# A decoder layer's MLP in blocks of 336 tokens, with the inner layer of its last 736 tokens as seven block products for eight, and GpSimd making a third of the low parts

## The reference

```
x = layer_norm(x, ln_in)
proj = x @ w_in                        # 1024 -> 9 * 256
y = [rg-lru, gated conv, stick-breaking attention, pooling](proj)   # 4 x 256
x = layer_norm(ALPHA * x + y @ w_out, ln1)
h = square(relu(x @ w_ff1))            # 1024 -> 4096
x = layer_norm(ALPHA * x + h @ w_ff2, ln2)     # 4096 -> 1024
```

## Time and profile before

| | |
|---|---|
| time, 3 runs | 2442.67, 2443.44, 2443.89 us |
| profiled execution | span 2440.8 us, 36,724 instructions; the page gives no time of its own beside the span |
| TensorE matmul / weight load, busy | 99% / 96% of the span |
| Vector, ScalarE, GpSimd, busy | 65%, 53%, 10% |
| DMA | 351.64 MB, 144 GB/s on average |
| block 0 begins, block 3 begins, block 4 begins | 527, 1696, 2130 us |

### The profile page before, as it was taken

The page is one execution under the profiler, slowest core; times in us unless marked ns, Lnnn a source line. Parts: engine busy times, 40 slices in busy tenths (PEclk is TensorE's granted clock), DMA queues, the critical chain, the costliest instruction groups (busy, mean ns, idle before and its releaser), DMA issues.

```text
span 2440.8 us, 36724 instructions
## 1 busy us (share of the span) xinstructions
PE 2406.7 (99%) x13263; PEld 2331.5 (96%) x13263; DVE 1585.0 (65%) x2233; ACT 1286.6 (53%) x1982; POOL 243.0 (10%) x527
## 2 busy tenths in 40 slices
PE   7999999999999999999999999999999999999998
PEld 7999999999999999999999999999999999999998
DVE  7635662656777787777788777757655665764335
ACT  5466523555655745656555565554455555444432
POOL 0012320200001100011100111000122130000000
PEclk9999999999999999999999999999999999999999
DMA  8434554534444434444443443333566674343332
GB/s 257 153 108 143 159 174 138 184 111 130 162 134 139 142 110 144 150 129 144 128 124 117 137 141 124 125 122 114 182 187 187 209 234 134 120 136 117 112 118 83
DMA packets 141526, 351.64 MB, mean 144 GB/s; under 512 B 20625, under 2 KB 64146, under 8 KB 141218
## 3 DMA queue, kind: packets, MB, share of 16 engines
q1 hardware_dynamic: 128994, 312.88, 40.6%
q0 software_dynamic: 12352, 36.42, 4.7%
HBM read 300.11 MB, written 49.12 MB: 143 GB/s over the span
## 4 chain that ended last, share of the span: by engine, by line
PE 95%; DVE 2%; ACT 2%; DMA 1%; issue 1%; SPq 0%; DVEq 0%; ACTq 0%
PE PS L1136 22%; PE PS L1138 22%; PE PS L1137 22%; PE PS L874 5%; PE PS L872 5%; PE PS L873 5%; PE PS L942 2%; PE PS L964 1%; PE PS L932 1%; PE PS L963 1%; PE PS L1026 1%; PE PS L933 1%; PE PS L1056 1%; PE PS L1014 1%; PE PS L912 1%
## 5 line engine op out<-in xcount | busy, mean ns | idle before, releaser
L1440 ACT ACTIVATE w_hi_lo<-w_raw 128x1024 fp32r<-128x1024 f32 x240 | 252.7, 1053 | 283.5 <-PE PS L1138 277.3
L1136 PE MATMUL PS<-a_hi,w_hi_lo 128*128 128x416 f32 x1080 | 385.1, 357 | 1.3 <-DVE w_hi_lo L1995 1.3
L1138 PE MATMUL PS<-a_hi,w_hi_lo 128*128 128x416 f32 x1080 | 379.3, 351 | 0.0
L1137 PE MATMUL PS<-a_lo,w_hi_lo 128*128 128x416 f32 x1080 | 378.6, 351 | 0.0
L1995 DVE TENSOR_TENSOR w_hi_lo<-w_raw,w_hi_lo 128x1024 fp32r<-128x1024 f32 x240 | 292.6, 1219 | 58.1 <-ACT w_hi_lo L1440 55.9
L1136 PE MATMUL PS<-h_hi,w_hi_lo 128*128 128x416 f32 x824 | 294.6, 358 | 0.0
L1138 PE MATMUL PS<-h_hi,w_hi_lo 128*128 128x416 f32 x824 | 290.2, 352 | 0.0
L1137 PE MATMUL PS<-h_lo,w_hi_lo 128*128 128x416 f32 x824 | 289.4, 351 | 0.0
L2022 DVE TENSOR_TENSOR h_lo<-h_full,h_hi 128x416 fp32r<-128x416 f32 x160 | 94.6, 592 | 222.9 <-ACT h_hi L1455 222.8
L1136 PEld LDWEIGHTS PS<-a_hi,w_hi_lo 128*128 128x128 f32 x1080 | 203.0, 188 | 4.1 <-DVE w_hi_lo L1995 1.7
L1137 PEld LDWEIGHTS PS<-a_lo,w_hi_lo 128*128 128x128 f32 x1080 | 203.5, 188 | 2.1
(11 more groups left out here) (336 smaller groups left out, 5203.8 us busy)
## 6 DMA issues: line engine op xcount, KB each, us to landing
w_raw<-w_all SPq DMA_DIRECT2D x380, 512.0 KB, 3.5
proj_scratch<-stage SPq DMA_DIRECT2D x70, 208.0 KB, 1.9
k_rows<-kv_out SPq DMA_DIRECT2D x80, 128.0 KB, 4.0
v_hi_lo<-v_scratch SPq DMA_DIRECT2D x40, 256.0 KB, 4.1
x_scratch<-x_full SPq DMA_DIRECT2D x20, 416.0 KB, 2.9
x_residual<-x_scratch SPq DMA_DIRECT2D x5, 1664.0 KB, 7.6
pages<-ck SPq DMA_DIRECT2D x64, 128.0 KB, 2.2
pages<-ck POOLq DMA_DIRECT2D x64, 128.0 KB, 2.5
```

Of the source, the lines that this page charges most:

```text
L1136: pe.matmul(out, w_h, mh_[:, k, :], start=(g == 0), stop=False)
L1137: pe.matmul(out, w_h, ml_[:, k, :], start=False, stop=False)
L1138: ins = pe.matmul(out, w_l, mh_[:, k, :], start=False, stop=(g == KT - 1))
L1440: act.activation(halves(w_hi(n)), raw_halves(n), ACT.Copy).then_inc(s_wh, 1)
```

## The change

**Blocks.** The MLP now has `NA` = 4 blocks of `MB` = 336 tokens, and a last part of 736 tokens that is two blocks (4 and 5) of `HB` = 368. Steps of blocks 0 to 3 are as before, but for their width. In block 3 the out steps of block 4 (r = 56 to 63) are followed by those of block 5 (r = 64 to 71), and the last eight down steps by nothing. So both normalisations run beside block 3's end. `N_STEPS` is 306. Rows of the second normalisation are 112 tokens, three tiles a block, at r = 1, 3 and 5.

**GpSimd.** `BY_POOL` lists every third step from 12 to 225. The low parts of those 72 weights are made by GpSimd, at the place of its list where the attention slot of that step is; its semaphore is its own (`s_wlp`), and TensorE and SP (`load_weights`) wait for it there.

**The last part.** For the up layer the weights of two output tiles and two halves of the contracted dimension form a 2 x 2 matrix of blocks, and so do the two halves of x with the two token blocks. Seven products of such blocks, with sums and differences of weights and of x as operands, and sums of products give what eight products gave. There are 8 chunks (`N_CH`), each with two units of seven up products (`b_up`), then eight weight tiles of the down layer, plain, with two groups each (`b_down`, `b_down_last`). A product or a group is 12 matmuls of 368 columns (`b_product`, `b_group`). GpSimd makes four sums of weights for each unit (`w_sums`) and one of x; Vector makes the other sums of x (`b_x_sum`), the low parts of 5 operands of x (`b_x_lo`, 1472 columns each) and of all weights (`b_lo`, 512 columns), and adds the products up (`b_add`); ScalarE copies products out of PSUM, makes the high parts and the last hidden sum. Six buffers hold parts of weights. The results are added to the residuals `xr` and `xr5` themselves. In the last chunk the groups of block 5 come first, and its rows are normalised beside those of block 4. The two half passes over the last three tiles are gone.

```diff
-    b, r = divmod(n - PRE, STEPS_B)
+    b, r = block_at(n)
...
-    if b < NB - 1 and r < 64:
-        return "out", b + 1, 0, r - 56
-    return "down", b, 3, r % 8
+    if r < 64 or (b == NA - 1 and r < 72):
+        return "out", b + 1 + (r - 56) // KT, 0, r % KT
+    return "down", b, 3, r % KT
...
+NA = 4
+MB = 336
+MNR, MROW = 3, 112
+HB = 368
+N_STEPS = PRE + NA * STEPS_B + KT
+RINGW = 6
+BY_POOL = [n for n in range(base_of(0) + 2, base_of(3)) if n % 3 == 0]
...
             def load_weights(n):
 
-                sp.wait_ge(s_wl, n + (NC_IN - 1))
+                wait_lo(sp, n - 2)
                 sp.dma_start(raw[:, n % 2, :], w_all[tile_at(n)]).then_inc(s_raw[n % 2], 16)
...
+            def up_load(u, o):
...
+                elif u % 2:
+                    sp.wait_ge(s_wl, WB + up_op(u - 1, 5 + o) + 1)
+                else:
+                    sp.wait_ge(s_wl, WB + down_op(u // 2 - 1, 5 + 2 * o) + 1)
+                sp.dma_start(raw[:, o, :], w_all[up_tile(4 * (u // 2) + u % 2 + 2 * o)]).then_inc(s_brq[2 * o], 16)
...
+            def b_up(u):
+
+                X, Y, Z = PS[:, 1 - u % 2, 0:HB], PS[:, 2, 0:HB], PS[:, 3, 0:HB]
...
+                for o in range(7):
+                    pe.wait_ge(s_wl, WB + up_op(u, o) + 1)
...
+                    elif u == 0:
+                        pe.wait_ge(s_xl, XB_DONE + o - 1)
+                    if o in (2, 4, 5):
+                        pe.wait_ge(s_bcopy, 3 * u + (1, 2, 3)[(2, 4, 5).index(o)])
+                    if o == 6:
+                        pe.wait_ge(s_badd, 3 * u + 2)
+                    out = (X, Y, X, Z, X, Z, X)[o]
...
+                    b_product(up_op(u, o), out, x_h, x_l, o in (0, 1, 3))
...
+                    else:
+                        pe.wait_ge(s_hl, FB + 8 * c + 7)
+                        b_group(c, m, 0, (0, 1, 2), bank + 1, True, False)
+                        b_group(c, m, 1, (0, 2, 3, 1), bank, True, True)
+                        pe.wait_ge(s_hl, FB + 8 * c + 8)
+                        b_group(c, m, 0, (3,), bank + 1, False, True)
...
-                if n >= N_STEPS:
+                if n >= N_STEPS or n in BY_POOL:
                     return
                 dve.wait_ge(s_wh, n + (NC_IN + 1))
...
+            def b_add(u, o):
+
+                which, bank = {1: (0, 2), 4: (1, 1 - u % 2), 5: (2, 3)}[o]
...
+                dve.tensor_tensor(h, h, PS[:, bank, 0:HB], ALU.add).then_inc(s_badd, 1)
+                wait_apart(dve, s_badd, done)
+                dve.scalar_tensor_tensor(out=h, in0=h, scalar=0.0, in1=h, op0=ALU.max, op1=ALU.mult).then_inc(s_r, 1)
...
+                    if b == 3 and r in (61, 62):
+                        split_y(5, 2 * (r - 61))
+                        split_y(5, 2 * (r - 61) + 1)
+                    for d, s in ((b + 1, r), (5, r - 8 if b == 3 else -1)):
...
+            for u in range(2 * N_CH):
+                for o in range(7):
+                    if o in (1, 4, 5):
+                        b_add(u, o)
+                    if o == 2:
+                        h_lo(u, 0)
+                    if u == 0 and o in (0, 1, 2):
+                        b_x_lo(o + 2)
+                    if o >= 5:
+                        h_lo(u, o - 4)
+                    b_prepare(up_event(u, o))
+                h_lo(u, 3)
...
+            for n in range(PRE, base_of(3)):
+                t = SLOT_AT.get(n, N_UNITS)
+                if t < N_UNITS and not unit(t)[3]:
+                    attention(t)
+                if n + 2 in BY_POOL:
+                    lo_ahead(n + 2)
+                if t < N_UNITS and unit(t)[3]:
+                    attention(t)
...
+            def w_sums(u):
+
+                c, j = divmod(u, 2)
+                for q in (0, 2):
+                    pool.wait_ge(s_brq[q], 16 * (4 * c + j + 1))
+                if u:
+                    pool.wait_ge(s_wl, WB + up_op(u - 1, 3) + 1)
+                pool.tensor_tensor(sc[:, 0, :], raw_part(2), raw_part(3), ALU.add).then_inc(s_bsum, 1)
+                wait_apart(pool, s_bsum, 4 * u + 1)
+                pool.tensor_tensor(sc[:, 1, :], sc[:, 0, :], raw_part(0), ALU.subtract).then_inc(s_bsum, 1)
+                pool.tensor_tensor(raw_part(2), raw_part(0), raw_part(2), ALU.subtract).then_inc(s_bsum, 1)
+                wait_apart(pool, s_bsum, 4 * u + 3)
+                pool.wait_ge(s_wl, WB + up_op(u, 1) + 1)
+                pool.tensor_tensor(raw_part(0), raw_part(1), sc[:, 1, :], ALU.subtract).then_inc(s_bsum, 1)
```

More of the change, by code:

```diff
@@ L2105, in last_rows @@
-                for m in between:
-                    token_half(1, m)
-                dve.wait_ge(s_std, NB + e + js[1] + 1)
-                own.up(dve.reciprocal(rstd[0:ROW, two], std[0:ROW, two]))
+                        row = rows_1[0:n, j, half * 512:half * 512 + 512]
+                        src = PS[0:n, 2 + j, :] if half else row
+                        own.up(dve.scalar_tensor_tensor(out=row, in0=src, scalar=mv[0:n, j, 0:1],
+                                                        in1=gb2[0:n, 0, half * 512:half * 512 + 512], op0=ALU.subtract, op1=ALU.mult))
@@ L2109, in last_rows @@
+                dve.wait_ge(s_std, NB + e + js[-1] + 1)
+                own.up(dve.reciprocal(rstd[0:n, cols], std[0:n, cols]))
                 own.sync()
@@ L2511, in _, with lo_ahead, attention @@
             pool.wait_ge(s_sn, 1)
[L2512 removed]
+            def lo_ahead(n):
+                pool.wait_ge(s_wh, n + (NC_IN + 1))
+                pool.tensor_tensor(halves(w_lo(n)), raw_halves(n), halves(w_hi(n)).bitcast(F32), ALU.subtract).then_inc(s_wlp, 1)
+            def attention(t):
                 v, i, w, top = unit(t)
```

949 lines of the change are left out of this document (667 added, 282 removed).

## The result

| | before | after |
|---|---|---|
| time, median (lowest to highest) | 2443.53 us (2442.67 to 2443.89) | 2501.72 us (2500.84 to 2504.53) |
| span of the profiled execution | 2440.8 us | 2500.4 us |
| ratio of after to before, 95% interval | | 1.0241, 1.0226 to 1.0255 |

What follows compares the result with a forecast made beforehand. TensorE was taken as the bound, busy for 99% of the 2440.8 us span, with Vector second. The terms -32.4 + 14 + 9 + 6.5 + 2 gave -0.9, so 2442.5 us, within no change; range 2421 to 2465.

Steps and rivals of the forecast that it cites:

- TensorE's saving: Whole kernel: fewer dense matmul columns, fewer transposes and cheaper narrow matmuls take 32.4 us off TensorE; bounds 27 and 37.
- 3 ns plus 0.444 ns a column: TensorE's assumed price of a matmul, giving 152.2 ns for 336 columns and 166.4 for 368.
- A narrow matmul that keeps 188 ns: Sign said to make everything wrong: the narrower matmuls on TensorE still taking 188 ns each.
- Costs, one: the hand-over: End of block 3 into the last part: TensorE waits for Vector's splits of x, 14 us; bounds 8 and 23.
- Two: inside the last part: Last part's 8 chunks: TensorE waits on the low part of h, plus slips, 9 us; bounds 4 and 18.
- slips: Last part: allowance of 0.3 us a chunk for weight sums that come just in time.
- Three: the end: After the last matmul: later row work puts the span's end about 19 us behind it, cost 6.5; bounds 3 and 9.
- Four: blocks 0 to 2: Shorter steps with GpSimd's 72 low parts cost 0.7 us a block, 2 in all; bounds 0 and 24.
- The second rival: The same as "The exclusion decides".
- The cover holds: Hand-over, chunks and end: Vector catches up and sums are in time, losses 20 us, 2429 us; chance 0.30.
- The exclusion decides: Blocks 0 to 2: GpSimd's 72 low parts block Vector, 22 us at 0.3 each, 2464 us; chance 0.28.
- Width does not pay: TensorE: matmuls bound by weight load near 188 ns, so 1,536 more would cost 289 us; chance 0.02.

Runs made afterwards that it cites:

- e3: Kernel after, with GpSimd's sums of weights and of x in the last part replaced by fills that read nothing (sums left out): 2489.3 us.
- e9: Kernel after, with low parts prepared from a unit's fourth product on placed behind additions in Vector's queue, and a TensorE wait before down products split: 2482.6 us.
- e1: Kernel after, with an empty list for GpSimd, so Vector makes all low parts of weights: 2496.8 us.
- e4: Kernel before, with GpSimd making every third low part of a weight in blocks 0 to 2: 2446.8 us.
- e2: Kernel after, with GpSimd's 72 low parts replaced by zero fills that read nothing (low parts left out): 2503.2 us.
- e5: Kernel after, with both late stores of V issued at step 10 and a block's three row stores two steps later: 2506.1 us.
- e11: e1 with the rows of the finished block taken at steps 1, 4 and 6 for 1, 3 and 5: 2496.7 us.
- e14: Kernel after, with both late stores of V issued at step 10 and nothing else: 2501.2 us.

## Why the prediction was wrong

The forecast saw no change where the kernel became slower, and missed it in the costs: 31.5 us were forecast and 85.9 measured, the largest miss in blocks 0 to 2, taken at 2 us and measured at 25.2. The saving was 6 us smaller than forecast.

**TensorE's saving, 32.4 forecast, 26.3 measured.** One step that failed is the line "3 ns plus 0.444 ns a column". Its 187.7 ns came from 325 matmuls in a window of 61.00 us, but a window also counts the matmuls that overlap its edges; from start to start it is 188.8. With 336 and 368 measured at 153.7 and 168.0 the line is about 7 ns plus 0.437. Narrower matmuls thus pay 1,536 x 7 ns, not x 3, and a dense saving forecast at 26.8 us is 20.5 (8,640 x 188.8 ns against 6,912 x 153.7 and 3,264 x 168.0). The lower bound of the forecast, 27 "if the 3 ns were 6", came close: it is 26.3 in all. (The excess of the 208-column matmuls is 0.0145 us each by the forecast's own line, not 0.016; that is 0.2 us.) "A narrow matmul that keeps 188 ns" was excluded rightly.

**Costs, one: the hand-over, 14 forecast, 27 measured.** The mechanism was right (Vector behind from step 61, TensorE waiting at the first x product), the size was not. At 1909 to 1932 about 7 us of waits and 2.9 at the lower clock; at 1958 to 1990 13.2 of waits and 4.0 at the lower clock: 27 in all, above the bound of 23. Two terms are the reason: the clash with GpSimd's sums, counted as 1.2 us, is 3.1 on one sum alone, and the waits at the first products are 13.2 us in the kernel after and 5.8 in e3; and the clock was left out altogether, at no price and with no reason given. The last 9 us of block 3's row belong to no term of the forecast: waits of 1.0 and 1.4 us at 1560 and 1566 with 2.3 us of lower clock behind them, 1.3 at 1847, and seven of the sample tokens' attention on `z_sample`, 2.7 in all. Before the change none of these was above 0.6; what makes them was not tested.

**Two: inside the last part, 9 forecast.** Each chunk loses 1.0 on the low part of h (forecast 0.8, though its own terms add up to 2.7 and not 2.8, so 0.7), the last one 1.3 on a weight's, and each but the first 1.35 on an addition (forecast 0.3 for "slips"): 17.9 in all. The tally said that the sums would be in time by half a microsecond; the margin was smaller than its error. e9 shows both to be queue order: I had taken the order of `b_prepare` and the wait for the seventh sum as given, and asked only whether the time sufficed.

**Three: the end, 6.5 forecast, 5.4 measured.** Right. The last dense matmul starts at 2482.30, 18.1 us before the end of the span, for 12.7.

**Four: blocks 0 to 2, 2 forecast, 25.2 measured.** This is the step that failed by most. Its upper bound of 24 stood nearly high enough, for the wrong reason. The second rival put its 22 us on GpSimd's 72 low parts; e1 and e4 give them 3 to 5, and in e2, where they read nothing, nothing came back. The forecast took 0.7 us a block and gave the latencies that a shorter step uncovers no other price. In the trace the waits of these blocks, less those of the kernel before, are some 15 of the 25.2 us and the lower clock is 4; some 6 show in no wait above 0.15 us. My account is that they come from latencies that a step of 4.5 us had covered and one of 3.7 does not. That one such wait grew from 1.3 to 4.5 us is shown, some 2 us of it without GpSimd. That it is so for the rest is argued from the kind of waits, not shown: e5, e11 and e14 could only move them, and no run has a step of another length with the same work beside it. How the 20 us that e1 leaves there divide stays open.

**The rivals.** "The cover holds" was wrong in every term but that of the end (5, measured 5.4): Vector's average spare time is no cover. "The exclusion decides" came nearest in time, at 2464, but its place was wrong: the exclusion works in the last part, for 12 us at most (e3), and nearly half of what the last part loses came back by reordering alone (e9). Nor does Vector overflow where that rival put it: block 1 loses 3.6 us of TensorE with GpSimd's low parts and 3.7 without (e1). "Width does not pay" was wrong as forecast.

All told the forecast erred by 6 us on the saving and 54 on the costs: 23 in blocks 0 to 2, some 13 at the hand-over (of its 27 the lower clock is 6.9), 9 in the chunks and 9 in block 3's early waits, less 1 at the end and 1.5 ahead of block 0, and nearly 3 in the last part that are assigned to none.

## What to carry to other kernels

A tiling that makes every step shorter takes cover from everything of fixed length: DMA latency, row work, a chain through three engines. List the chains that end in one step and compare each with the new step, not the engines' averages. In an in-order queue ask of each instruction what stands ahead of it that waits for a slow producer: here 19 us of 58 came back by moving such low parts behind the addition and splitting one wait, while three repairs in the full stretches moved the wait and gained nothing that the medians resolve. And work handed to another engine does not always relieve the first: Vector was busy for 284.65 us in block 1 with GpSimd's help and for 281.88 without.

## What I had not expected of the hardware

- A wait of TensorE can cost more than its length: behind 8.4 us of idling the granted clock was 0.50 for 6 us, 2.5 us more, and behind 3.5 us still 1.5 more, at 1983 to 1986. It need not: after the same 3.3 us at 533 e11 ran at 0.50 and e1 did not. The mean granted clock is 0.989 for 0.997 before.
- Fills of GpSimd that read nothing cost the kernel as much as the subtractions they replace (e2, 2503.2 against 2501.7 us), though Vector's product beside them fell from 1075 ns to 695. Sums that became fills gave 12.4 us back (e3), where TensorE waits for the chain.
- The price of a matmul is a straight line from 336 to 416 columns with about 7 ns at its foot, once it is read from start to start.
